# A hybrid two-layer decoder on one core: the order of transposes, products and low halves in the second layer's first norm

## Chip, cores and metric

One Trainium2 chip, one of its cores. The metric is the device time of one launch in microseconds (us), as the median of several runs. A second number appears beside it: the span of one profiled execution, from its first instruction to its last, which is a little shorter than that execution's own time.

## What is computed

512 tokens of width 1024 go through two layers, each a mixer and a mixture of experts, each with a norm ahead and a residual sum behind. The place of the change is the seam between the two layers:

```
h = rms_norm(x, norm_ffn_w[0])
x = x + hierarchical_moe(h, ...)      # each token: two experts, two weights
h = rms_norm(x, norm_mix_w[1])
mix = retention_mixer(h, ...)         # begins with h @ w_in, 1024 x 6144
```

All products are in float32 accuracy: each operand is split into a rounded high part and the low part that is left, and three matmuls (high by high, low by high, high by low) replace one.

## The kernel before

The kernel is written engine by engine, in one fixed order for each; engines meet only at semaphores. The tokens are 4 tiles of 128 (T = 0 to 3). Weights come as pieces: SyncE loads 512 KB, ScalarE makes the high half (L1006), GpSimd or VectorE the low half (L840, L1761).

**The seam, step by step.** Each token's two expert results lie in HBM, scattered there by GpSimd. ScalarE issues the loads of them, tile by tile (L1343 to L1346). For each tile these steps follow:

1. VectorE adds the two weighted results into the residual `x`: `combine`, two instructions (L1469). The second raises `moe_added0`.
2. TensorE waits for that, and transposes the tile: 8 transposes of 128x128 into two PSUM banks (L2144).
3. ScalarE writes the high half of the transposed tile, scaled with the norm's weights: 8 instructions of 128x128 (`transposed`, L1029). It also sums the squares of the tile's rows (`square`, L1020).
4. VectorE writes the low half: 8 instructions (`lo_tiles`, L1572). The first four can start once ScalarE's first four are done, since the two banks are handed over one by one.
5. TensorE multiplies the tile with the first weight block of the retention input (`rows(10, T)`): four pieces of 6 matmuls each, 24 in all (L673 to L675). It waits for the whole low half of the tile.

The norm's root isn't applied here; it is applied to the products later on, so the products don't wait for it. The roots are made while the products run: GpSimd turns each sum of squares into a root (L855, L856), ScalarE makes four diagonal matrices of them (`roots`, L1062), issues three small loads (L1370), prepares three weight pieces (L1006) and then evacuates the first block's products (L1242), followed by VectorE (L1820). The next block's first product waits for that.

**Orders around the change.** A tile's low half is L(T), its combines C(T), its transposes X(T), its products of pieces 0 to 2 P(T), of piece 3 Q(T). TensorE's order before is: 22 filler matmuls, X0, X1, 3 fillers, P0, X2, Q0, P1, X3, Q1, then P2 Q2 P3 Q3, roots. The fillers (`keep_busy`, L2111; each is two matmuls in the trace) compute nothing that is used. VectorE's order is C0 C1 L0 C2 L1 C3 L2 L3. ScalarE's is: high halves of 0, of 1, square 0, high halves of 2, square 1, high halves of 3, squares 2 and 3.

Each `hT` tile takes two of four PSUM banks in turn (`open_tile`), so a tile's transposes also wait until the low half of the tile two before it has been made.

Of the kernel before, what the change touches and what calls it, by code (L numbers as in the profile page):

```python
# [32 lines left out]
NT = SEQ // P  # L33
# [33 lines left out]
MOE_AT = (10, 26)  # L67
# [4 lines left out]
def first_piece(db):  # L72

    return 4 * db + (6 * NE if db >= MOE_AT[0] else 0)
# [248 lines left out]
def build(nc, a, out):  # L323
    ctx = ExitStack()
    with ctx:
# [3 lines left out]
        def sem(name):  # L329
            return ctx.enter_context(nc.semaphore(name))  # L330
# [39 lines left out]
        def v3(ap, k):  # L370
            return ap.rearrange("p (k n) -> p k n", k=k)
# [119 lines left out]
        def fin(T):  # L491
            return reg(DM * T, DM)
# [19 lines left out]
        def s_(name):  # L512
            if name not in SEM:
                SEM[name] = sem(name)
            return SEM[name]
# [90 lines left out]
        def tile(name):  # L606
            return ps[:, 4 + SIDE_AT[name] % 4, :]

        def tile_is_ready(eng, name):
            eng.wait_ge(tile_ready, SIDE_AT[name] + 1)  # L610
# [57 lines left out]
        def cols(T, w=P):  # L668
            return slice(T * w, T * w + w)
# [327 lines left out]
        def _(act):  # L997
# [24 lines left out]
            def transposed(n, T):  # L1022
                for g in range(2):
                    name = ("hT", n, T, g)
                    tile_is_ready(act, name)
                    if n == 2:
                        for j in range(4):
                            k = 4 * g + j
                            A(act.activation(HTH[:, k, cols(T)], tile(name)[:, cols(j)], ACT.Copy, scale=nw1[:, k:k + 1]),  # L1029
                              s_("hT_hi_made") if j == 3 else None)  # L1030
                        continue
                    A(act.activation(HTH[:, 4 * g:4 * g + 4, cols(T)], v3(tile(name), 4), ACT.Copy), s_("hT_hi_made"))

            def norm(n):
                if n == 2:
                    act.wait_ge(s_("wb_loaded"), 32)
                    transposed(n, 0)
                    for T in range(NT):
                        if T + 1 < NT:
                            transposed(n, T + 1)  # L1040
                        square(n, T)
                    roots()
                    return
                if n == 4:
                    for T in range(NT):
                        square(n, T)
                    return
                for T in range(3):
                    square(n, T)
                transposed(n, 0)  # L1050
                hi(0)
                square(n, 3)
                transposed(n, 1)
                transposed(n, 2)
                hi(1)
                transposed(n, 3)
                hi(2)
# [383 lines left out]
        def _(dve):  # L1441
# [24 lines left out]
            def combine(l, T, j):  # L1466

                dve.wait_ge(s_("yp_second0" if T == 0 and j == 1 else f"yp_loaded{T}"), 16 * (l + 1))
                D(stt(X[:, T, :], YP[:, T, j, :], w12[:, 2 * T + j:2 * T + j + 1], X[:, T, :], ALU.mult, ALU.add),  # L1469
                  s_(f"moe_added{l}") if j == 1 else None)  # L1470

            def norm(n):
                if n == 2:
                    for i in range(4):
                        lo(first_piece(10) + i)
                    combine(0, 0, 0)
                    combine(0, 0, 1)
                    combine(0, 1, 0)
                    combine(0, 1, 1)
                    dve.wait_ge(s_("wb_loaded"), 32)  # L1480
                    for T in range(NT):
                        lo_tiles(("hT", n, T), T)
                        if T + 2 < NT:
                            combine(0, T + 2, 0)
                            combine(0, T + 2, 1)
                    return
                if n == 4:
                    def last(T):
                        dve.wait_ge(s_("norm_r"), 16 + T + 1)
                        D(stt(fin(T), X[:, T, :], rs[:, T:T + 1], wb(4), ALU.mult, ALU.mult), s_("fin_dve"))  # L1490

                    for T in range(NT):
                        for j in range(2):
                            combine(1, T, j)
                        if T == 2:
                            dve.wait_ge(s_("wb_loaded"), 64)
                            last(0)
                    last(1)
                    last(2)
                    dve.wait_ge(s_("norm_r"), 16 + 4)  # L1500
                    for hf in range(2):
                        c = slice(512 * hf, 512 * hf + 512)
                        D(stt(fin(3)[:, c], X[:, 3, c], rs[:, 3:4], wb(4)[:, c], ALU.mult, ALU.mult), s_("fin_dve"))
                    return
                def scale(T):
                    dve.wait_ge(s_("norm_r"), T + 1)
                    D(stt(htok(0)[:, T, :], X[:, T, :], rs[:, T:T + 1], wb(0), ALU.mult, ALU.mult), s_("h_ready"))

                dve.wait_ge(s_("wb0_loaded"), 16)
                scale(0)  # L1510
                scale(1)
                lo_tiles(("hT", n, 0), 0)
                scale(2)
                lo_tiles(("hT", n, 1), 1)
                scale(3)
                lo_tiles(("hT", n, 2), 2)
                lo_tiles(("hT", n, 3), 3)
# [45 lines left out]
            def lo_tiles(name, T):  # L1563

                for g in range(2):
                    nm = name + (g,)
                    dve.wait_ge(s_("hT_hi_made"), hT_hi_count(nm))
                    hi, lo = (x[:, 4 * g:4 * g + 4, cols(T)] for x in ((HTH2, HTL2) if name[0:3] == ("yT", 1, 0) else (HTH, HTL)))
                    if name[0:2] == ("hT", 2):
                        for j in range(4):  # L1570
                            k = 4 * g + j
                            ins = stt(lo[:, j, :], tile(nm)[:, cols(j)], nw1[:, k:k + 1], hi[:, j, :].bitcast(F32), ALU.mult, ALU.subtract)  # L1572
                            if j < 3:
                                D(ins)
                            else:
                                D.read(ins, nm)
                    elif name[0:2] == ("yT", 0):
                        D.read(stt(lo, v3(tile(nm), 4), head_w[:, g:g + 1], hi.bitcast(F32), ALU.mult, ALU.subtract), nm)
                    else:
                        D.read(tt(lo, v3(tile(nm), 4), hi.bitcast(F32), ALU.subtract), nm)  # L1580
# [506 lines left out]
        def _(pe):  # L2087
# [20 lines left out]
            def keep_busy(count):  # L2108

                for _ in range(count):  # L2110
                    mm(ps[:, 0, 0:5 * CH], ident[:, :], gm.rearrange("p m t -> p (m t)"), start=True, stop=True)  # L2111
# [18 lines left out]

            def norm(n):
                if n == 2:
                    keep_busy(22)
                for T in range(NT):
                    if n == 2:
                        pe.wait_ge(*x_ready(n, T))
                    else:
                        pe.wait_ge(s_("h_ready"), h_count(n, T))
                    row = X[:, T, :] if n == 2 else htok(n)[:, T, :]
                    for g in range(2):  # L2140
                        t = open_tile(("hT", n, T, g))
                        for j in range(4):
                            k = 4 * g + j
                            ins = tr(t[:, cols(j)], row[:, k:DM:KD], ident[:, :])  # L2144
                        done(ins)
                    if n == 0 and T < 2:
                        stay_warm((4, 6)[T])
                    if n == 0 and T == 2:
                        stay_warm(4)
                        piece0(0, (0, 1))  # L2150
                    if n == 2:
                        if T == 1:
                            keep_busy(3)
                        if T > 1:
                            rows(MOE_AT[0], T - 2, (3,))
                        if 0 < T < NT - 1:
                            rows(MOE_AT[0], T - 1, (0, 1, 2))
                if n == 0:
                    piece0(0, (2, 3))
                    piece0(1, (0, 1, 2, 3)).then_inc(piece_used, 1)  # L2160
                if n == 2:
                    rows(MOE_AT[0], 2)
                    rows(MOE_AT[0], 3)

            def roots():
                pe.wait_ge(s_("rs_diag"), NT)
# [648 lines left out]
```

## Time and profile before

| | |
|---|---|
| median of 3 runs | 1178.06 us (1177.57 to 1178.78) |
| the profiled execution's own time | 1180.1 us |
| its span | 1178.3 us |
| TensorE busy | 1111.0 us, 94% |
| mean granted TensorE clock | 0.974 of full |
| VectorE, ScalarE, GpSimd busy | 59%, 52%, 34% |

The rows below write an engine as PE (TensorE matmuls), PEld (its weight loads), DVE (VectorE), ACT (ScalarE), POOL (GpSimd), SP (SyncE). L2144 is line 2144 of the kernel. In a timeline, one row merges equal instructions that follow one another: start, duration of the whole row, engine, line, operation, output and inputs, count; in square brackets the idle time of the engine ahead of it and what ended that. Matmul ends are modelled, so a matmul's rate is read from the starts of two that follow each other.

### The profile page before, as it was taken

What the parts mean: (1) busy time and instruction counts of PE and PEld (TensorE: products, weight loads), DVE (VectorE), ACT (ScalarE), POOL (GpSimd) and SP (SyncE); (2) the same over time, 40 slices, a digit from 0 to 9 for tenths busy, and PEclk for the clock granted to TensorE, in tenths of its full rate; (3) what the DMA queues carried; (4) which work ended last, traced back from release to release, by engine and by line L of the source; (5) the groups of instructions that cost most, each with busy time, mean ns of one, the idle gap of its engine ahead of it and who ended that gap; (6) DMA issues with size and microseconds to landing.
All of it is one profiled execution on the core that took longest, in us unless ns stands there. A gap on an engine that the chain in (4) does not pass through costs nothing.

```text
span 1178.3 us, 19724 instructions
## 1 busy us (share of the span) xinstructions
PE 1111.0 (94%) x7062; PEld 912.4 (77%) x7063; DVE 699.3 (59%) x1016; ACT 608.7 (52%) x903; POOL 395.7 (34%) x344
## 2 busy tenths in 40 slices
PE   8999999999998899998999999999999997999990
PEld 5778887778787688886788888888888886788870
DVE  5435444368736999996646341543432138999975
ACT  5556234242434699995633342233342234899971
POOL 4343221110133244332155325442234442344332
PEclk8999999999999899999999999999999998999995
DMA  9333311112225699996443213331222364999945
GB/s 263 77 88 55 73 38 55 36 41 70 72 64 210 244 358 379 382 365 225 181 128 98 81 56 106 94 108 58 81 73 90 98 198 161 355 381 377 381 191 223
DMA packets 81668, 194.76 MB, mean 165 GB/s; under 512 B 20349, under 2 KB 21433, under 8 KB 80825
## 3 DMA queue, kind: packets, MB, share of 16 engines
q1 hardware_dynamic: 59368, 159.34, 40.2%
q10 hardware_dynamic: 12432, 17.60, 4.4%
q0 software_dynamic: 9792, 16.80, 3.8%
q8 instruction: 49, 0.80, 0.3%
q14 instruction: 27, 0.21, 0.1%
HBM read 189.50 MB, written 23.07 MB: 180 GB/s over the span
## 4 chain that ended last, share of the span: by engine, by line
PE 83%; DVE 7%; DMA 3%; ACT 3%; issue 1%; ACTq 1%; POOL 0%; POOLq 0%; DVEq 0%
PE ps L673 24%; PE ps L675 23%; PE ps L674 23%; PE ps L2572 2%; PE ps L2364 2%; DMA arena<-y 1%; DVE x L1469 1%; PE ps L2247 1%; ACTq L1423 1%; PE ps L2500 1%; DMA arena<-hs,slot_rows 1%; PE ps L2637 1%; PE ps L2201 1%; ACT wh L1006 1%; DMA y<-arena,cur_rows 1%
## 5 line engine op out<-in xcount | busy, mean ns | idle before, releaser
L840 POOL TENSOR_TENSOR wl<-raw,wh 128x1024 fp32r<-128x1024 f32 x94 | 228.6, 2440 | 380.4 <-ACT wh L1006 380.1
L673 PE MATMUL ps<-wh,hT_hi 128*128 128x512 f32 x864 | 347.3, 402 | 2.9 <-DVE hT_lo L1988 2.4
L675 PE MATMUL ps<-wh,hT_lo 128*128 128x512 f32 x864 | 338.4, 392 | 0.0
L674 PE MATMUL ps<-wl,hT_hi 128*128 128x512 f32 x864 | 337.9, 391 | 0.0
L1006 ACT ACTIVATE wh<-raw 128x1024 fp32r<-128x1024 f32 x116 | 122.4, 1068 | 213.0 <-PE ps L675 191.3
L673 PEld LDWEIGHTS ps<-wh,hT_hi 128*128 128x128 f32 x864 | 163.1, 189 | 38.1 <-DVE hT_lo L1988 2.9
L675 PEld LDWEIGHTS ps<-wh,hT_lo 128*128 128x128 f32 x864 | 162.6, 188 | 34.5
L674 PEld LDWEIGHTS ps<-wl,hT_hi 128*128 128x128 f32 x864 | 163.0, 189 | 30.7
L673 PE MATMUL ps<-hT_hi,wh 128*128 128x512 f32 (+1 forms) x296 | 117.0, 395 | 2.0 <-DVE arena_rounded L1820 1.0
L1963 DVE TENSOR_TENSOR wl<-arena,wh 128x1024 fp32r<-128x1024 f32 x96 | 113.6, 1222 | 5.6 <-ACT wh L1293 5.3
L674 PE MATMUL ps<-hT_lo,wh 128*128 128x512 f32 (+1 forms) x296 | 114.5, 387 | 0.0
L675 PE MATMUL ps<-hT_hi,wl 128*128 128x512 f32 (+1 forms) x296 | 114.4, 387 | 0.0
L1963 DVE TENSOR_TENSOR wl<-raw,wh 128x1024 fp32r<-128x1024 f32 x92 | 109.2, 1223 | 7.7 <-ACT wh L1293 6.2
L1293 ACT ACTIVATE wh<-arena 128x1024 fp32r<-128x1024 f32 x94 | 98.4, 1070 | 6.9 <-PE ps L675 5.8
L1293 ACT ACTIVATE wh<-raw 128x1024 fp32r<-128x1024 f32 x84 | 88.1, 1072 | 5.2 <-PE ps L675 4.1
L673 PEld LDWEIGHTS ps<-hT_hi,wh 128*128 128x128 f32 x296 | 56.0, 189 | 15.7 <-issue 2.0
L675 PEld LDWEIGHTS ps<-hT_hi,wl 128*128 128x128 f32 x296 | 56.1, 189 | 11.4
L674 PEld LDWEIGHTS ps<-hT_lo,wh 128*128 128x128 f32 x296 | 56.0, 189 | 10.3
L885 POOL COPY cur_rows<-slot_rows 128x1 uint32 (+1 forms) x32 | 6.6, 206 | 139.6 <-PE ps L2572 139.6
L851 POOL TENSOR_TENSOR small<-small 128x4 f32<-128x4 f32 (+1 forms) x10 | 14.5, 1448 | 98.4 <-DVE small L1699 98.4
L1955 DVE TENSOR_TENSOR hT_lo<-ps,hT_hi 128x512 fp32r<-128x512 f32 x64 | 41.1, 683 | 0.6 <-ACT hT_hi L1351 0.5
L1020 ACT ACTIVATE arena<-x 128x1024 f32<-128x1024 f32 x20 | 21.2, 1058 | 37.3 <-DVE x L1469 18.2
(331 smaller groups left out, 1581.1 us busy)
## 6 DMA issues: line engine op xcount, KB each, us to landing
raw<-in_moe_w_gate_up_dram SPq DMA_DIRECT2D x64, 512.0 KB, 9.7
arena<-in_moe_w_gate_up_dram SPq DMA_DIRECT2D x64, 512.0 KB, 9.6
raw<-in_odd_w_in_dram SPq DMA_DIRECT2D x48, 512.0 KB, 3.8
raw<-in_even_w_in_dram SPq DMA_DIRECT2D x32, 512.0 KB, 4.8
arena<-in_moe_w_down_dram SPq DMA_DIRECT2D x32, 512.0 KB, 10.1
raw<-in_moe_w_down_dram SPq DMA_DIRECT2D x32, 512.0 KB, 12.8
raw<-in_odd_w_out_dram SPq DMA_DIRECT2D x16, 512.0 KB, 3.5
arena<-y ACTq DMA_DIRECT2D x6, 1024.0 KB, 9.8
```

The costliest lines, as they stand in the source:

```text
L673: nc.tensor.matmul(dst, lh, rh, start=first, stop=False)
L674: nc.tensor.matmul(dst, lh, rl, start=False, stop=False)
L675: return nc.tensor.matmul(dst, ll, rh, start=False, stop=last)
L840: pool.tensor_tensor(columns_of(i, wl[:, i % NSPL, :, :]), raw_columns(i), columns_of(i, wh[:, i % NSPL, :, :]).bitcast(F32), ALU.subtract ...
L851: pool.tensor_tensor(dst, src, mhalf[:, 0:n], ALU.pow).then_inc(on, 1)
L1006: act.activation(columns_of(i, wh[:, i % NSPL, :, :]), raw_columns(i), ACT.Copy).then_inc(hi_done, 1)
L1020: A(act.activation(squares(n), X[:, T, :], ACT.Square, scale=DM ** -0.5, accum_out=ss[:, T:T + 1]), s_("norm_ss"))
L1293: act.activation(wh[:, n % NSPL, :, :], raw_at(in_turn(n, it)), ACT.Copy).then_inc(hi_done, 1)
L1955: tt(HTL[:, 2 * par + g, :], ps[:, 4 + g, :], HTH[:, 2 * par + g, :].bitcast(F32), ALU.subtract).then_inc(s_("xT_lo"), 1)
L1963: tt(wl[:, n % NSPL, :, :], raw_at(in_turn(n, it)), wh[:, n % NSPL, :, :].bitcast(F32), ALU.subtract).then_inc(lo_dve, 1)
L2364: blocks(name, lambda o, b, n: mm(o, of_block(lh, b, n), of_block(rh, b, n), start=True, stop=True))
L2572: ins = tr(ps[:, 4 + g, cols(j)], xg[:, par, 4 * g + j:DM:KD], ident[:, :])
```

## The change

VectorE makes the low half of tile 0 right after tile 0's combines, ahead of tile 1's. TensorE no longer transposes tile T+1 ahead of tile T's products: it runs pieces 0 to 2 of tile T-1, then tile T's transposes, then piece 3 of tile T-1. ScalarE takes the square of a tile right after that tile's high halves. The fillers become 20 and 5 in place of 22 and 3.

```diff
@@ ScalarE
                     act.wait_ge(s_("wb_loaded"), 32)
-                    transposed(n, 0)
                     for T in range(NT):
-                        if T + 1 < NT:
-                            transposed(n, T + 1)
+                        transposed(n, T)
                         square(n, T)
                     roots()
@@ VectorE
-                    combine(0, 0, 0)
-                    combine(0, 0, 1)
-                    combine(0, 1, 0)
-                    combine(0, 1, 1)
-                    dve.wait_ge(s_("wb_loaded"), 32)
                     for T in range(NT):
-                        lo_tiles(("hT", n, T), T)
-                        if T + 2 < NT:
-                            combine(0, T + 2, 0)
-                            combine(0, T + 2, 1)
+                        combine(0, T, 0)
+                        combine(0, T, 1)
+                        dve.wait_ge(s_("wb_loaded"), 32)
+                        if T > 1:
+                            lo_tiles(("hT", n, T - 1), T - 1)
+                        elif T == 0:
+                            lo_tiles(("hT", n, 0), 0)
+                    lo_tiles(("hT", n, NT - 1), NT - 1)
                     return
@@ TensorE
                 if n == 2:
-                    keep_busy(22)
+                    keep_busy(20)
                 for T in range(NT):
+                    if n == 2 and T > 0:
+                        rows(MOE_AT[0], T - 1, (0, 1, 2))
                     if n == 2:
                         pe.wait_ge(*x_ready(n, T))
@@
                     if n == 2:
-                        if T == 1:
-                            keep_busy(3)
-                        if T > 1:
-                            rows(MOE_AT[0], T - 2, (3,))
-                        if 0 < T < NT - 1:
-                            rows(MOE_AT[0], T - 1, (0, 1, 2))
+                        if T == 0:
+                            keep_busy(5)
+                        else:
+                            rows(MOE_AT[0], T - 1, (3,))
@@
                 if n == 2:
-                    rows(MOE_AT[0], 2)
-                    rows(MOE_AT[0], 3)
+                    rows(MOE_AT[0], NT - 1)
```

TensorE's order is now: 20 fillers, X0, 5 fillers, P0, X1, Q0, P1, X2, Q1, P2, X3, Q2, P3 Q3, roots. Its queue at the start of the seam, before (L2111 are the fillers, L2144 the transposes, L673 the first product of a tile):

```order
L2111 MATMUL ps<-half_masks,ident 128x320 x22
L2144 MATMUL ps<-ident,x 128x128 x16
L2111 MATMUL ps<-half_masks,ident 128x320 x3
L673 MATMUL ps<-wh,hT_hi 128x512
L674 MATMUL ps<-wl,hT_hi 128x512
L675 MATMUL ps<-wh,hT_lo 128x512
```

and with the change, where the fillers stand at L2108 and the transposes at L2143:

```order
L2108 MATMUL ps<-half_masks,ident 128x320 x20
L2143 MATMUL ps<-ident,x 128x128 x8
L2108 MATMUL ps<-half_masks,ident 128x320 x5
L673 MATMUL ps<-wh,hT_hi 128x512
L674 MATMUL ps<-wl,hT_hi 128x512
L675 MATMUL ps<-wh,hT_lo 128x512
```

Tile 1's 8 transposes have gone from ahead of the first product to behind the 18th; those of tiles 2 and 3 each moved behind 24 more products than before.

VectorE's queue in the seam, before (L1469 are the combines, L1572 the low halves, L1820 the next block's):

```order
L1469 SCALAR_TENSOR_TENSOR x<-arena,small,x 128x1024 x4
L1572 SCALAR_TENSOR_TENSOR hT_lo<-ps,vec,hT_hi 128x128 x8
L1469 SCALAR_TENSOR_TENSOR x<-arena,small,x 128x1024 x2
L1572 SCALAR_TENSOR_TENSOR hT_lo<-ps,vec,hT_hi 128x128 x8
L1820 SCALAR_TENSOR_TENSOR arena_rounded<-ps,small,arena_rounded 128x512 x4
```

and with the change (L1467 the combines, L1569 the low halves, L1817 the next block's):

```order
L1467 SCALAR_TENSOR_TENSOR x<-arena,small,x 128x1024 x2
L1569 SCALAR_TENSOR_TENSOR hT_lo<-ps,vec,hT_hi 128x128 x8
L1467 SCALAR_TENSOR_TENSOR x<-arena,small,x 128x1024 x4
L1569 SCALAR_TENSOR_TENSOR hT_lo<-ps,vec,hT_hi 128x128 x8
L1817 SCALAR_TENSOR_TENSOR arena_rounded<-ps,small,arena_rounded 128x512 x4
```

Only one group moved: the low half of tile 0 and the combines of tile 1 have changed places. From tile 1's low half on, the two queues are the same.

## Rows read from the trace of the kernel before

**Rows 1.** The page's chain that ended last, by engine.
```profile
PE 83%; DVE 7%; DMA 3%; ACT 3%; issue 1%; ACTq 1%; POOL 0%; POOLq 0%; DVEq 0%
```

**Rows 2.** Chain of waits through the seam's start: start, us, what.
```profile
551.89 8.31 DMA arena<-y
...
560.29 1.30 DVE x L1469
```

**Rows 3.** Timeline of the seam, PE, DVE and ACT.
```profile
548.11 12.11 PE L2111 MATMUL ps<-half_masks,ident 128*128 128x320 f32 x44 [1.83 <-issue]
...
556.54 2.60 DVE L1469 SCALAR_TENSOR_TENSOR x<-arena,small,x 128x1024 f32<-128x1024 f32 x2 [4.01 <-DMA arena<-y]
...
560.06 1.04 PE L2144 MATMUL ps<-ident,x 128*128 128x128 f32 x8
...
562.93 3.06 DVE L1572 SCALAR_TENSOR_TENSOR hT_lo<-ps,vec,hT_hi 128x128 fp32r<-128x128 f32 x8
...
562.95 1.16 PE L2144 MATMUL ps<-ident,x 128*128 128x128 f32 x8 [1.85 <-DVE x L1469]
...
566.04 0.50 PE L673 MATMUL ps<-wh,hT_hi 128*128 128x512 f32 x1 [0.32 <-DVE hT_lo L1572]
...
570.28 1.04 PE L2144 MATMUL ps<-ident,x 128*128 128x128 f32 x8
...
571.07 0.48 PE L673 MATMUL ps<-wh,hT_hi 128*128 128x512 f32 x1
...
576.64 1.04 PE L2144 MATMUL ps<-ident,x 128*128 128x128 f32 x8
577.34 3.17 ACT L1029 ACTIVATE hT_hi<-ps,vec 128x128 fp32r<-128x128 f32 x8 [2.01 <-PE ps L2144]
...
579.00 3.11 DVE L1572 SCALAR_TENSOR_TENSOR hT_lo<-ps,vec,hT_hi 128x128 fp32r<-128x128 f32 x8 [1.55 <-ACT hT_hi L1029]
```

**Rows 4.** Timeline behind the last tile's high halves, up to the next block's first product.
```profile
581.71 1.06 ACT L1020 ACTIVATE arena<-x 128x1024 f32<-128x1024 f32 x1
...
583.90 1.71 ACT L1062 ACTIVATE arena<-ident,small 128x128 f32<-128x128 f32 x4 [1.03 <-POOL small L856]
...
587.05 3.17 ACT L1006 ACTIVATE wh<-raw 128x1024 fp32r<-128x1024 f32 x3 [1.44 <-issue]
...
589.79 1.05 PE L2169 MATMUL ps<-arena,small 128*128 128x128 f32 x8
590.12 2.84 ACT L1242 ACTIVATE arena_rounded<-ps,small 128x512 fp32r<-128x512 f32 x4
...
591.80 0.47 PE L673 MATMUL ps<-hT_hi,wh 128*128 128x512 f32 x1 [0.95 <-DVE arena_rounded L1820]
```

**Rows 5.** Timeline of PE at two idle stretches elsewhere.
```profile
314.48 0.66 PE L2527 MATMUL ps<-arena 64*64 64x128 f32 x8 [1.76 <-DVE state L1755]
...
991.40 1.68 PE L2572 MATMUL ps<-ident,arena 128*128 128x128 f32 x8 [2.02 <-DMA arena<-hs,slot_rows]
```

**Rows 6.** Windows of 1 us: PE busy, its instructions, granted clock, DMA share, GB/s.
```profile
316.00:317.00 1.00, 0.81 (x8) 0.51 0.05 20
992.00:993.00 1.00, 1.00 (x7) 0.50 0.14 57
562.00:563.00 1.00, 0.05 (x1) 1.00 0.84 352
```

**Rows 7.** Timeline of PE at half clock: first two products, and the first one behind.
```profile
80.72 0.63 PE L674 MATMUL ps<-hT_lo,wh 128*128 128x512 f32 x1
81.14 0.63 PE L675 MATMUL ps<-hT_hi,wl 128*128 128x512 f32 x1
...
84.03 0.39 PE L673 MATMUL ps<-hT_hi,wh 128*128 128x512 f32 x1
```

**Rows 8.** Window of 100 us behind the seam, PE, columns as in rows 6.
```profile
592.00:692.00 100.00, 100.00 (x456) 1.00 0.33 100
```

**Rows 9.** Waits of PE from 592 to 1150, the largest: us, times, longest.
```profile
PE ps L2227 <- DVE arena L1868: 3.0, 2, 2.6
```

## The prediction

> **What bounds the kernel now.** I read the page's chain first: TensorE holds 83% of it [rows 1], so outside the seam the kernel goes at TensorE's pace. Then the chain through the seam, where it leaves TensorE. It runs through the loads of the expert results, whose last link before the norm ends at 560.2, when tile 1's results are there [rows 2]; then through tile 1's combines (560.29 to 562.90), tile 0's low half (562.93 to 565.99) and on to the first product at 566.04 [rows 3]. So the first product waits for VectorE, which does tile 1's combines ahead of tile 0's low half. The change takes that away. From 566.04 TensorE never stops until 589.79, when it reaches the roots' matmuls [rows 3, 4].
>
> The reader should see two more things. **First, what hides a tile's latency.** From the start of a tile's transposes to its finished low half three engines work in turn. For the last tile, where nothing else is in the way: transposes at 576.64, ScalarE from 577.34 to 580.51, VectorE from 579.00 to 582.11 [rows 3]. That is 5.47 us, and with the 0.06 us from a low half's end to the product that waits for it 5.53 us. TensorE doesn't feel it now, because between tile T's transposes and its products stand 24 products of the two tiles before it. **Second, a second chain.** After the last transposes ScalarE has the high halves, two squares (the last starts at 581.71), the roots (583.90), three loads to issue, three weight pieces (587.05) and only then the first evacuation at 590.12, with the next block's first product at 591.80 [rows 4]. The pieces run back to back (3.17 us for three), so at the end of the seam it is ScalarE that is late, by the 0.95 us that TensorE waits there.
>
> **The terms.** A tile's first 18 products after a wait take 570.28 - 566.04 = 4.24 us [rows 3]. Behind transposes the first product starts 571.07 - 570.28 = 0.79 us after their start. From tile 3's transposes to the roots' matmuls stand 6 + 24 + 24 = 54 products, so one takes (589.79 - 576.64 - 0.79) / 54 = 0.229 us [rows 3, 4].
>
> *The start, a gain.* Tile 0's combines end at 559.14 [rows 3]. Before, its transposes came only at 560.06, held up by the 22 fillers (44 matmuls from 548.11, 0.27 us each). With 20 the fillers end at about 559.0, and the transposes start at 559.19 (the 0.05 us is what tile 1's show: combines end 562.90, transposes 562.95). Tile 0's low half is next in VectorE's queue, so the first product comes at 559.19 + 5.53 = 564.72. Gain so far: 566.04 - 564.72 = 1.32 us. The 5 new fillers take 10 x 0.27 = 2.7 us of this wait and leave some 1.8 us idle, as before (1.85 ahead of 562.95).
>
> *The low half and the combines, change places.* Combines of tile 1: about 564.7 to 567.3, of tile 2 to 569.9, of tile 3 behind tile 1's low half. Each tile is summed before its transposes' turn comes, as below. That the later low halves still stand behind a combine costs nothing: tile 1's can't start before 571.3, and VectorE is free at 569.9.
>
> *The transposes behind the products, the large term.* Tile T's transposes now start 4.24 us after tile T-1's first product. Between them and tile T's first product only 6 products stand. Transposes and these take 0.79 + 6 x 0.229 = 2.2 us, but the low half needs 5.53 us. TensorE idles 5.53 - 2.2 = 3.3 us, three times. A tile's period is 4.24 + 5.53 = 9.77 us, against 6.36 us before (576.64 - 570.28).
>
> | | transposes | first product |
> |---|---|---|
> | tile 0 | 559.19 | 564.72 |
> | tile 1 | 568.96 | 574.49 |
> | tile 2 | 578.73 | 584.26 |
> | tile 3 | 588.50 (before 576.64) | 594.03 |
>
> Tile 3's 24 products end at 594.03 + 0.11 + 24 x 0.229 = 599.6, where 589.79 was (0.11: what a first product after a wait takes longer).
>
> *The end of the seam.* ScalarE's chain hangs on tile 3's transposes, 11.86 us later. It gets one square back: tile 2's now stands ahead of tile 3's high halves, so the last square comes right behind them, 0.70 + 3.17 + 0.02 = 3.89 us after the start of the transposes, at 592.39: 10.68 us after its 581.71. Roots, loads and pieces follow as before, since none of the three pieces waits for TensorE longer: the last needs tile 3's piece 2 done at about 598.4, and ScalarE comes to it at 599.8. The next block's first product is at 591.80 + 10.68 = 602.48. TensorE's own path (599.6, then 1.05 us of roots' matmuls) is 1.8 us shorter, so ScalarE's decides. **Shift: +10.7 us**, at a full clock.
>
> *The clock.* Rows show the granted clock falling to half of full (1.2 in place of 2.4 GHz) around idle stretches of 1.76 and 2.02 us [rows 5, 6], and not around the 1.85 us ahead of 562.95 [rows 3, 6]. At half clock a product takes 81.14 - 80.72 = 0.42 us in place of 0.23; that stretch ended by 84.03, after (84.03 - 80.72) / 0.42 = some eight products [rows 7], and so cost 8 x 0.2 = 1.6 us. Each of the new stalls is longer than every one of these, so the clock will likely fall. Bounds: nothing, and 1.6 us for each fall. I take 1.2 us, nearer the upper end, since a fall that begins within the idle time has less work left to slow. Two of the three count (ahead of tile 1's and tile 2's products): the third delays tile 3's products alone, where TensorE has 1.8 us to spare. **+2.4 us.**
>
> The Trainium skill, page "TensorE: Matmul & The Clock Gate", section "Why this matters for your kernels", speaks against this change: it tells to leave no long idle gap between bursts of matmuls, because the array then goes back to half rate. By that rule both stalls on the path would be paid in full, 3.2 us in place of my 2.4, as in the second rival below. The trace agrees in part: of the three idle stretches named, two brought the clock down.
>
> *Behind the seam nothing gives it back.* TensorE is busy for 100.00 us of the next 100 [rows 8], and its waits up to the last experts are short and for VectorE, which moves along [rows 9]. The transfers of the expert results were issued before the seam and hang on nothing that moved; the weight loads wait for buffers that TensorE and GpSimd free, and so move with the rest.
>
> **Sum.** 10.7 + 2.4 = 13.1 us. The profiled execution took 1180.1 us and would take 1193.2; it lies 2.0 us above the median, so against the median: 1178.06 + 13.1 = **1191.2 us**.
>
> **Rivals.**
> - *Full clock.* The stalls come, the clock stays. For it: 1.85 us of idle time did nothing, with transposes on both sides. Against: 3.3 us is longer than all of those. 1178.06 + 10.7 = 1188.7.
> - *Both falls at full price.* Each fall begins only when the products run again, and slows some eight of them: 2 x 1.6 = 3.2 us, 1178.06 + 10.7 + 3.2 = 1192.0. For it: at 316 and 992 the clock was at half while TensorE was busy again [rows 6]. Against: the idle stretches here are longer, so more of the half clock may fall into them. (This is the time that the skill's rule gives.)
> - *Half clock throughout.* Once down, the clock doesn't recover within a tile. The 18 products ahead of the transposes of tiles 2 and 3 would take 18 x 0.2 = 3.6 us more each, the transposes a little too: 10.7 + 8 = 18.7, 1196.8. Against: a stretch at half clock ended after some eight products while TensorE stayed busy [rows 7], and a tile has 24.
> - *Not slower: the delay is taken up behind the seam.* If weights or buffers, not TensorE, set the pace of the retention blocks, work ahead would gather during the stalls, and TensorE would catch up. It decides where TensorE waits for at least 10.7 us, from 592 on, on something that doesn't move with it; then 1178.1, or 1176.7 with the early start. The rows have it at 0 in the next 100 us, and at 3.0 us for the largest of its later waits.
> - *The change doesn't reach what it says.* VectorE's queue changes in one place only, as its rows show. If that were all that counts, TensorE's earlier start would be the whole effect: -1.3 us, 1176.7. It would need a latency behind a tile's transposes below 2.2 us, where the rows have 5.53.
>
> **How the numbers follow.** Stalls with falls of the clock that are paid in part: 0.46, my forecast. Both at full price: 0.30. Full clock: 0.16. Half clock throughout: 0.03. Not slower, by either way: 0.04. The last 0.01 is for a large miss upwards. The range takes in full clock, less 1.2 us for my sum being made of single rows (1187.5), and reaches up to three falls on the path at full price (10.7 + 4.8 = 15.5) with 0.6 for the sum: 1194.2. Some 2 us, 0.2%, is about what a measurement of this kernel can tell from no change. Slower by more 0.96, within it 0.03, faster by more 0.01.
>
> **What the profile would show.** Right: first product at 564.7; three idle stretches of 3.3 us ended by the low half, so some 10 us of waits of TensorE's first product for it, where 0.3 stood; tile 3's transposes at 588.5 or up to 3 us later; the next block's first product at 602.5 to 605.5; windows at half clock between 570 and 600. Wrong: if TensorE's stalls are well below 3 us each, the latency of a tile isn't what I read; if the shift at the next block's first product is some 12 us but the time grows by less, something behind the seam had slack.

## The result, and the profile after

| | before | after |
|---|---|---|
| median | 1178.42 us (1177.57 to 1187.04, 4 runs) | 1195.15 us (1192.99 to 1197.99, 4 runs) |
| ratio after to before | | 1.0131, 95% interval 1.0105 to 1.0157 |
| span of the profiled execution | 1178.3 us | 1191.3 us |
| mean granted clock | 0.974 | 0.972 |

The change makes the kernel slower by 1.3%: 15.4 us by the ratio (12.4 to 18.5 by its interval), 16.7 us by the difference of the two medians. I forecast 13.1 us. On the 1178.06 us that I forecast from, the ratio gives 1193.5 us, inside my range; the plain median of the four runs lies 1.0 us above its upper end (1194.2). The four times stand in two pairs, 1193.0 and 1193.1 against 1197.2 and 1198.0; their mean clocks are 0.973 and 0.972 against 0.965 and 0.965. That is a first sign that the clock has a larger part in the time than my sum gave it.

The profiled execution took 1193.1 us, where I had put 1193.2. That is luck: its seam lost more than my sum said, and the rest of this execution took less, as the traces show next.

The timeline of the seam after the change, all engines (columns as in rows 3 and 4; the whole trace stands 2.8 us earlier here, see below):

```profile
553.75 2.61 DVE L1467 SCALAR_TENSOR_TENSOR x<-arena,small,x 128x1024 f32<-128x1024 f32 x2 [4.23 <-DMA arena<-y]
...
556.42 1.16 PE L2143 MATMUL ps<-ident,x 128*128 128x128 f32 x8 [0.29 <-DVE x L1467]
...
562.06 0.50 PE L673 MATMUL ps<-wh,hT_hi 128*128 128x512 f32 x1 [1.79 <-DVE hT_lo L1569]
...
566.30 1.04 PE L2143 MATMUL ps<-ident,x 128*128 128x128 f32 x8
...
571.84 0.80 PE L673 MATMUL ps<-wh,hT_hi 128*128 128x512 f32 x1 [3.10 <-DVE hT_lo L1569]
...
578.82 1.05 PE L2143 MATMUL ps<-ident,x 128*128 128x128 f32 x8
...
584.36 0.61 PE L673 MATMUL ps<-wh,hT_hi 128*128 128x512 f32 x1 [3.10 <-DVE hT_lo L1569]
...
590.20 1.05 PE L2143 MATMUL ps<-ident,x 128*128 128x128 f32 x8
590.90 3.17 ACT L1029 ACTIVATE hT_hi<-ps,vec 128x128 fp32r<-128x128 f32 x8 [7.03 <-PE ps L2143]
...
595.74 0.80 PE L673 MATMUL ps<-wh,hT_hi 128*128 128x512 f32 x1 [3.10 <-DVE hT_lo L1569]
...
605.68 0.47 PE L673 MATMUL ps<-hT_hi,wh 128*128 128x512 f32 x1 [0.56 <-DVE arena_rounded L1817]
```

The reader should see three first products, each with 3.10 us of idle time ahead of it that a low half ends. In [rows 3, 4] TensorE ran from 566.04 to the roots without a stop. TensorE's waits in the seam say the same in one row (us in total, times, longest), where [rows 3] had 0.32 us:

```profile
PE ps L673 <- DVE hT_lo L1569: 11.1, 4, 3.1
```

To compare traces that begin the seam at different times I measure from the start of tile 0's transposes to the next block's first product, **the stretch** from here on: 591.80 - 560.06 = 31.74 us before, 605.68 - 556.42 = 49.26 us after. My table had 602.48 - 559.19 = 43.3 us for it at full clock. What lies between 43.3 and 49.3 is the clock, as experiments 2 and 3 show. Windows of 1 us of TensorE after the change (length, busy time and instructions, granted clock, DMA share, GB/s), at the first and at the second of the three stalls:

```profile
570.00:571.00 1.00, 0.00 (x0) 0.97 1.05 385
571.00:572.00 1.00, 0.16 (x1) 0.50 0.99 365
...
576.00:577.00 1.00, 1.00 (x4) 0.50 0.00 0
577.00:578.00 1.00, 1.00 (x4) 0.62 0.00 0
...
584.00:585.00 1.00, 0.64 (x2) 0.80 0.02 8
585.00:586.00 1.00, 1.00 (x3) 0.50 0.00 0
...
587.00:588.00 1.00, 1.00 (x4) 0.50 0.00 0
588.00:589.00 1.00, 1.00 (x5) 1.00 0.00 0
```

The clock falls at 570.9, while TensorE is idle, and comes back at 577.8: 6.8 us. At the second stall it falls at 584.6, just after the products have started, and comes back at 588.0: 3.4 us.

**The rest of the trace.** The seam's first row stands at 553.75 in place of 556.54. The first layer lost less here: the two stretches that the clock spent at half there before, one from 80.7 to 84.0 [rows 7] and one at 316 [rows 6], aren't in this trace, though nothing was changed there. Behind the seam, from the next block's first product to the second layer's router (the matmul at L2227 before, L2223 after, that follows a wait of 0.46 us), it takes 976.52 - 591.80 = 384.72 us before and 990.40 - 605.68 = 384.72 us after. Nothing of the delay is given back up to there. The row before:

```profile
976.52 0.19 PE L2227 MATMUL ps<-arena 128*128 128x32 bf16 x1 [0.46 <-DVE arena L1868]
```

and after:

```profile
990.40 0.19 PE L2223 MATMUL ps<-arena 128*128 128x32 bf16 x1 [0.46 <-DVE arena L1865]
```

From there to the end it takes 201.8 us before and 200.9 us after. So the 13.0 us between the two spans are 2.8 us less ahead of tile 0's combines, 51.93 - 35.26 = 16.7 us more from these to the next block's first product, and 0.9 us less at the end.

### The profile page after: what moved, and what is told of

It reads as the page before. It is cut to its first block, busy times and chain, and to the rows that moved or that the text cites. A ratio compares the mean times of both kernels' runs of the same rounds, so it can differ in the third digit from the quotient of the medians.

```text
span 1191.3 us, 19726 instructions
## 1 busy us (share of the span) xinstructions
PE 1114.0 (94%) x7063; PEld 913.1 (77%) x7063; DVE 699.2 (59%) x1016; ACT 609.0 (51%) x903; POOL 397.5 (33%) x344
## 4 chain that ended last, share of the span: by engine, by line
PE 84%; DVE 7%; DMA 3%; ACT 2%; issue 2%; ACTq 1%; POOLq 0%; POOL 0%; DVEq 0%; SPq 0%
PE ps L673 24%; PE ps L675 23%; PE ps L674 23%; PE ps L2568 2%; PE ps L2360 2%; PE ps L2197 1%; DMA arena<-y 1%; DVE hT_lo L1569 1%; DVE x L1467 1%; PE ps L2243 1%; ACTq L1421 1%; DMA arena<-hs,slot_rows 1%; PE ps L2496 1%; DMA x<-in_x_dram 1%; PE ps L2633 1%
## 5 line engine op out<-in xcount | busy, mean ns | idle before, releaser
L673 PE MATMUL ps<-wh,hT_hi 128*128 128x512 f32 x864 | 349.8, 405 | 13.8 <-DVE hT_lo L1569 11.1
L673 PEld LDWEIGHTS ps<-wh,hT_hi 128*128 128x128 f32 x864 | 164.3, 190 | 51.0 <-DVE hT_lo L1569 12.9
L673 PE MATMUL ps<-hT_hi,wh 128*128 128x512 f32 (+1 forms) x296 | 116.3, 393 | 2.2 <-issue 0.9
L673 PEld LDWEIGHTS ps<-hT_hi,wh 128*128 128x128 f32 x296 | 55.6, 188 | 15.9 <-issue 2.2
```

The source lines that it names most:

```text
L673: nc.tensor.matmul(dst, lh, rh, start=first, stop=False)
```

## Experiments

Theory A, from the prediction: three stalls of some 3 us and the second chain, on ScalarE, cost 10.7 us, and the rest of the loss is TensorE's clock, which the stalls bring down. Each experiment's times are compared with runs of the kernel before that were taken together with them.

**1. The changed kernel again.** No edit.

> The changed kernel once more, for a second trace of the same program. Theory A (stalls of 3.1 us, three of them, and a clock that falls in each): the seam, from tile 0's combines to the next block's first product, takes 51.9 us as in the first trace if the clock falls at the same points, and down to 46.0 us (35.3 + 10.7) where it doesn't; run times come in groups some 3 to 5 us apart, with the mean clock lower in the longer ones. Rival B (the order alone costs all of it, whatever the clock): the seam is 51.9 us again within 0.3, and the groups come from elsewhere in the kernel.

1193.39 us (1192.43 to 1198.09, 4 runs), ratio 1.0118 (1.0079 to 1.0157). The stretch takes 604.05 - 557.74 = 46.31 us, 3 us less than in the first trace of the same program, with stalls of 3.09 us each. (From tile 0's combines, as I put it in advance, it is 50.4 us; there the second load of tile 0 came 1.5 us late, which is why I measure from the transposes.) What differs is the clock: two low stretches of 3.4 us, and none at the third stall. Rival B falls. An idle stretch of 3.09 us can leave the clock alone, as this trace shows at tile 3:

```profile
595.62 0.50 PE L673 MATMUL ps<-wh,hT_hi 128*128 128x512 f32 x1 [3.09 <-DVE hT_lo L1569]
```

```profile
593.00:594.00 1.00, 0.00 (x0) 1.00 0.00 0
594.00:595.00 1.00, 0.00 (x0) 1.00 0.00 0
596.00:597.00 1.00, 1.00 (x6) 1.00 0.00 0
```

**2. Fillers in the stalls.** The changed kernel, with 5 fillers into a PSUM bank that is free there, behind each tile's piece 3:

```diff
-            def keep_busy(count):
+            def keep_busy(count, bank=0):
...
-                    mm(ps[:, 0, 0:5 * CH], ident[:, :], ...)
+                    mm(ps[:, bank, 0:5 * CH], ident[:, :], ...)
...
                         else:
                             rows(MOE_AT[0], T - 1, (3,))
+                            keep_busy(5, 3)
```

> Fillers in the three stalls keep TensorE busy for 2.7 of 3.1 us, in the same order of the products; nothing else changes. Theory A: full clock from 560 to 606, tile 1's first product 9.8 us after tile 0's, the seam at 46.0 us, the kernel 10.7 to 11 us above before (1189.0 against 1178.2), and runs closer together. Rival B: the fillers change nothing, since the stalls are the waits for the low halves: the seam stays near 51.9 us and the kernel at 1193 to 1198.

1190.12 us (1187.79 to 1192.43, 6 runs), ratio 1.0078 (1.0053 to 1.0102): 9.2 us slower than before, with 6 to 12 in the interval. The stretch takes 603.29 - 559.92 = 43.37 us, with no window below full clock in it. So the loss at full clock is 43.4 - 31.7 = 11.6 us in this stretch, of which the earlier transposes of tile 0 (0.9 us) are taken off again: 10.7. That part of the sum stands to a tenth in the trace, and the runs' 9.2 us allow it. From tile 0's combines it is 603.29 - 554.37 = 48.9 us and not 46.0, since in this trace the 20 fillers began at half clock (from 547.5 to 551) and held tile 0's transposes back by 2.9 us. Rival B falls: the stretch is 3 to 6 us shorter than without fillers. The run times did not draw closer, which I had expected: they spread over 4.6 us here, and the kernel before over 7.8 us on this chip (1177.16 to 1184.99).

**3. Fewer fillers.** 3 in place of 5 in each stall, `keep_busy(3, 3)`.

> 3 fillers (1.6 us) in place of 5 in each of the three stalls, so that about 1.5 us of each stays idle, less than every idle stretch that has brought the clock down so far. Theory A: the clock stays full through the seam or falls once at most, and from tile 0's transposes to the next block's first product it takes 43.3 us as with 5 fillers (49.3 and 46.3 in the two traces without any). Rival D (any idle stretch ahead of products can bring the clock down, whatever its length): falls behind two or three of the stalls again, 45 to 49 us.

1189.84 us (1188.93 to 1190.67, 4 runs), ratio 1.0077 (1.0052 to 1.0102). Timeline and windows of TensorE in this kernel, at tile 1 and behind the last stall:

```profile
574.11 0.50 PE L673 MATMUL ps<-wh,hT_hi 128*128 128x512 f32 x1 [1.48 <-DVE hT_lo L1569]
...
602.06 0.47 PE L673 MATMUL ps<-hT_hi,wh 128*128 128x512 f32 x1 [1.84 <-DVE arena_rounded L1817]
```

```profile
574.11:578.33 4.22, 4.22 (x19) 1.00 0.05 17
593.60:602.06 8.46, 6.62 (x32) 1.00 0.31 95
```

The stretch takes 602.06 - 558.72 = 43.34 us at full clock throughout, and from tile 0's combines 602.06 - 556.05 = 46.01 us, where 35.3 + 10.7 = 46.0 had been put down. Idle stretches of 1.48 us, three in a row, left the clock alone. Rival D isn't borne out; experiment 7 gives three more such stretches.

**4. TensorE's order undone.** The changed kernel with the old `norm` on TensorE (22 fillers, X0, X1, 3 fillers, P0, X2, Q0, ...); VectorE and ScalarE as changed.

> TensorE's order as before (22 fillers, both transposes, 3 fillers, products), with the new orders of VectorE and ScalarE. Theory A: the loss is TensorE's order; here tile 1's transposes wait for tile 1's combines, now behind tile 0's low half, to about 567.4 on the clock of the first trace, and the first product comes near 569.9 against 566.04; no stalls behind it; the seam takes 38.2 us, 2.9 more than before, of 1181 us in all. Rival C (VectorE's new order is what costs, by holding back tiles 1 to 3): the seam stays above 45 us.

1186.37 us (1182.64 to 1188.29, 10 runs), ratio 1.0050 (1.0034 to 1.0067): 5.9 us slower than before, twice what I had expected. From tile 0's combines to the next block's first product it takes 596.47 - 555.52 = 40.95 us, where 38.2 was put down. TensorE's timeline and two of its windows in this kernel:

```profile
567.26 1.97 PE L2141 MATMUL ps<-ident,x 128*128 128x128 f32 x8 [7.13 <-DVE x L1467]
569.03 2.38 PE L2108 MATMUL ps<-half_masks,ident 128*128 128x320 f32 x6
571.00 0.64 PE L673 MATMUL ps<-wh,hT_hi 128*128 128x512 f32 x1
```

```profile
563.00:564.00 1.00, 0.00 (x0) 0.70 0.04 16
569.00:570.00 1.00, 1.00 (x4) 0.50 1.04 401
```

Tile 1's transposes come 8.17 us after tile 0's (8.16 by the sum), so what I had read of VectorE's order is right. The missing 2.75 us have three parts. TensorE is idle for 7.13 us ahead of them, the clock falls at 563.4 and is back at 570.2, and transposes and fillers take 3.74 us where my sum had 2.5: 1.2 us. I had worked that idle stretch out and not asked what it does to the clock. The 22 fillers hold tile 0's transposes to 3.57 us after its combines, as in the kernel before, where I had taken the 2.65 of 20 fillers: 0.9 us. And ScalarE's weight pieces wait for TensorE behind the last products, as in experiment 11: 0.6 us. No stalls follow, so rival C falls; yet it has a point: VectorE's new order fits only with TensorE's new one. With TensorE's old order, and ScalarE's new one, which alone shows in no run time (experiment 11), it costs 5.9 us.

**5. Transposes behind 6 products.** A tile's transposes stand behind piece 0 of the tile before, with pieces 1 to 3 behind them:

```diff
                     if n == 2 and T > 0:
-                        rows(MOE_AT[0], T - 1, (0, 1, 2))
+                        rows(MOE_AT[0], T - 1, (0,))
...
                         else:
-                            rows(MOE_AT[0], T - 1, (3,))
+                            rows(MOE_AT[0], T - 1, (1, 2, 3))
```

> A tile's transposes stand behind 6 of the products of the tile before it, in place of 18; 18 products follow them, in place of 6. Theory A: the stall shrinks from 3.1 us by 12 x 0.229 = 2.75 us to some 0.4 us for tiles 2 and 3 (tile 1's transposes also wait about 1.1 us for its combines), the clock stays full, tile 3's transposes come some 4.8 us later than before and the seam takes 35.3 + 3.6 = 38.9 us; kernel near 1182. Rival B' (it is enough that products stand ahead of transposes at all): the stalls stay near 3 us and the seam above 45 us.

1182.82 us (1179.51 to 1184.81, 10 runs), ratio 1.0015 (0.9999 to 1.0032). Timeline of TensorE in this kernel:

```profile
567.82 1.16 PE L2143 MATMUL ps<-ident,x 128*128 128x128 f32 x8 [0.99 <-DVE x L1467]
...
573.56 0.50 PE L673 MATMUL ps<-wh,hT_hi 128*128 128x512 f32 x1 [0.47 <-DVE hT_lo L1569]
...
580.62 0.50 PE L673 MATMUL ps<-wh,hT_hi 128*128 128x512 f32 x1 [0.39 <-DVE hT_lo L1569]
...
587.69 0.50 PE L673 MATMUL ps<-wh,hT_hi 128*128 128x512 f32 x1 [0.38 <-DVE hT_lo L1569]
```

The stalls are 0.47, 0.39 and 0.38 us where 0.4 was forecast, and tile 1's transposes wait 0.99 us for their combines where 1.1 was. The stretch takes 596.14 - 559.64 = 36.50 us (38.9 less the 2.65 us up to the transposes: 36.2 expected). From the combines it is 42.1 us, since the 20 fillers began at half clock in this trace and held tile 0's transposes back. So it is the number of products behind a tile's transposes that decides: 12 more of them take 2.7 us off each stall, and 10 us off the kernel, the clock's part with it. The stretch is still 36.50 - 31.74 = 4.8 us longer than before, 3.9 with tile 0's earlier transposes taken off; the runs show 1.8 us, with 0.1 faster to 3.8 slower in the interval. Why it is at the upper end of that stays open.

**6. VectorE's order undone, 5 fillers in each stall.** The `norm` of VectorE as before, the rest as in 2.

> As with 5 fillers in each stall, but VectorE's order as before: tile 1's combines ahead of tile 0's low half. Theory A: this order is worth the early start alone; from the start of tile 0's combines to tile 0's first product 9.5 us as in the kernel before (8.3 in the changed one), and three periods of 9.8 us behind it as with the new order. Rival C (VectorE's order has a part in the stalls): the periods come out shorter than 9.8 us.

One run, 1189.93 us. The periods between first products are 9.81, 9.79 and 9.80 us. The first term doesn't come out of this trace: the fillers began at half clock here too, held tile 0's transposes to 559.12, and the first product came 11.1 us after the combines, as in 2. Inconclusive for the early start, so I repeated it with 3 fillers.

**7. The same with 3 fillers in each stall.**

> 3 fillers in each stall, and VectorE's order as before the change (tile 1's combines ahead of tile 0's low half). Theory A: if the 20 fillers at the start run at full clock, tile 0's first product comes 9.5 us after its combines begin, as in the kernel before, where the new order had 8.3 us; three periods of 9.8 us behind it, and 44.6 us from tile 0's transposes to the next block's first product, 1.3 more than with the new order. Rival C (VectorE's order has a part in the stalls): periods below 9.8 us.

One run, 1191.38 us, at full clock through the seam. First product 564.26 - 554.78 = 9.48 us after the start of the combines; with the new order it was 562.06 - 553.75 = 8.31. The stretch takes 602.10 - 557.44 = 44.66 us, 1.3 more than in 3. Both as put down: the new place of tile 0's low half is worth 1.2 to 1.3 us, and no more. Rival C falls. The three stalls with fillers keep 1.49 us of idle time each, and the clock stays full again.

**8. to 10. Three more traces of the changed kernel**, for a rule on the clock that the first two traces suggested.

> The changed kernel, one more look at its three stalls. From two traces: a stall of 3.1 us brings the clock down five times in six; where it falls within 0.5 us of the first product or behind it, the low stretch lasts 3.2 to 3.5 us and the 18 products take 5.6 to 5.8 us in place of 4.2; where it falls 0.8 us or more ahead of the first product, the low stretch lasts 6.6 us and they take 7.0 us. Theory F: the same rule holds in this trace, for each stall. Rival G: the long stretches come without regard to where the clock fell.

> As the look before, the same two theories: 5.6 to 5.8 us for 18 products behind a late fall, 7.0 us behind an early one, 4.2 us without one (F), or no such order (G).

> As the two looks before, the same two theories (F and G), with the same numbers.

1197.69, 1192.22 and 1197.43 us. All fifteen stalls of the five traces of this program, with the time at which the clock fell, against the first product behind the stall (read from windows of 0.2 us), and how long it stayed at half:

| trace | tile 1 | tile 2 | tile 3 | the stretch |
|---|---|---|---|---|
| first | 0.90 ahead, 6.8 us | 0.24 behind, 3.4 us | 0.90 ahead, 6.8 us | 49.26 us |
| again | 0.66 behind, 3.4 us | 0.45 ahead, 3.4 us | no fall | 46.31 us |
| again2 | 1.05 ahead, 6.8 us | 0.15 behind, 3.4 us | 0.97 ahead, 6.8 us | 49.14 us |
| again3 | 0.39 ahead, 3.4 us | no fall | 0.85 ahead, 6.8 us | 46.34 us |
| again4 | 0.03 ahead, 3.4 us | 1.13 ahead, 6.8 us | 0.11 behind, 3.4 us | 47.92 us |

Thirteen falls in fifteen stalls. Every fall that came 0.85 us or more ahead of the first product lasted 6.8 us, every other one 3.4. Theory F holds in all, G falls. What a fall costs shows between a first product and the next transposes, which is 4.22 to 4.27 us without one: 5.60 to 5.84 us behind a short fall, 6.87 to 6.98 behind a long one. So 1.4 to 1.6 us, or 2.6 to 2.8. Behind the last stall, windows over the stretch to the next block's first product, in the first trace:

```profile
595.74:605.68 9.94, 9.38 (x32) 0.70 0.38 117
```

Against the 8.46 us of kernel 3 a long fall there costs 1.5 us; a short one cost 0.3 (608.04 - 599.27 = 8.77 in the last trace). How it gets through, in ScalarE's timeline of the first trace:

```profile
599.43 1.13 ACT L1006 ACTIVATE wh<-raw 128x1024 fp32r<-128x1024 f32 x1 [1.44 <-PE ps L675]
601.32 1.14 ACT L1006 ACTIVATE wh<-raw 128x1024 fp32r<-128x1024 f32 x1 [0.76 <-PE ps L675]
602.97 1.14 ACT L1006 ACTIVATE wh<-raw 128x1024 fp32r<-128x1024 f32 x1 [0.51 <-PE ps L675]
```

The three weight pieces no longer run back to back as in [rows 4]; the second and the third wait 0.76 and 0.51 us for TensorE's products of tile 3 that free their buffers, and the evacuation is queued behind them.

**11. One part of the change put into the kernel before.** ScalarE alone: tile 2's square ahead of tile 3's high halves.

```diff
-                    transposed(n, 0)
-                    for T in range(NT):
-                        if T + 1 < NT:
-                            transposed(n, T + 1)
-                        square(n, T)
+                    transposed(n, 0)
+                    transposed(n, 1)
+                    for T in range(NT):
+                        if T == 3:
+                            transposed(n, T)
+                        square(n, T)
+                        if T == 0:
+                            transposed(n, 2)
```

> The kernel before, with one thing of the change: ScalarE takes the square of tile 2 ahead of tile 3's high halves instead of behind them. Theory A: ScalarE's chain at the end of the seam gets 1.2 us shorter, TensorE's becomes the longer one, and the next block's first product comes 0.9 us earlier (30.8 us after tile 0's transposes in place of 31.7); the kernel 0.9 us faster, less than the runs can tell. Rival E (ScalarE's chain isn't what the next block waits for): nothing moves, 31.7 us.

1178.84 us (12 runs), ratio 0.9990 (0.9974 to 1.0006). The stretch takes 591.43 - 560.09 = 31.34 us, 0.4 us less than before; I had put down 0.9. ScalarE in this kernel:

```profile
585.99 1.12 ACT L1006 ACTIVATE wh<-raw 128x1024 fp32r<-128x1024 f32 x1 [1.54 <-PE ps L675]
587.35 1.14 ACT L1006 ACTIVATE wh<-raw 128x1024 fp32r<-128x1024 f32 x1 [0.24 <-PE ps L675]
588.71 1.14 ACT L1006 ACTIVATE wh<-raw 128x1024 fp32r<-128x1024 f32 x1 [0.22 <-PE ps L675]
```

The pieces wait for TensorE again, and the evacuation behind them gains only part of the 1.2 us. The chain is the one I named, so rival E falls, but the time is no different from before by what the runs can tell. No version here beats the kernel before clearly.

## Why the prediction was right, and where it was too small

The mechanism was right: three stalls for the low half, ScalarE's chain at the end, and a clock that falls. One term of the sum was too small, the clock's.

- **The early start.** Forecast 1.32 us, measured 9.50 - 8.31 = 1.19. Right. The missing 0.1 us: ScalarE's first high half starts 557.23 - 556.42 = 0.81 us after transposes that follow idle time, not 0.70 as after the others.
- **The stalls.** Forecast three of 3.3 us, measured three of 3.10. From a tile's transposes to its first product 5.53 us forecast, 5.54 measured (571.84 - 566.30); the period 9.77 us forecast, 9.75 at full clock (574.11 - 564.36 in kernel 3). Right.
- **ScalarE's chain as the one that ends last.** Forecast 43.3 us for the stretch at full clock, measured 43.34 and 43.37. Right, and with the early start taken off, 10.7 us. (Between a tile's transposes and its products stood 24 products before the change only for tile 1; for tiles 2 and 3 it was 30. The prediction's 24 enters no sum.)
- **Nothing is given back behind.** 384.72 us before and after, and 384.7 to 384.8 in every other trace. The rival on the other side falls.
- **The clock.** Here my sum failed. The step was "I take 1.2 us, nearer the upper end, since a fall that begins within the idle time has less work left to slow". The five traces show the reverse: a fall well ahead of the products is the dear one, since the clock then stays low for 6.8 us, and it costs 2.7 us, more than the 1.6 that I had as the upper bound. A short fall costs 1.5. The bound came from one low stretch of 3.3 us [rows 7], and in the 3 us ahead of it TensorE had no idle time, but ran 64 matmuls of one column each. The second step, "the third delays tile 3's products alone, where TensorE has 1.8 us to spare", held for a short fall (0.3 us) but not for a long one (1.5 us), because ScalarE's weight pieces wait for these same products. The prediction says that these pieces don't wait for TensorE, which by its own numbers holds only up to some 1.4 us of delay (599.8 against 598.4). In place of 2.4 us the clock took 5.9, 3.0, 5.8, 3.0 and 4.6 us in the five traces (the stretch less 43.3), 4.5 on the mean.
- **The size.** 10.7 + 4.5 = 15.2 us, against the 15.4 that the ratio of the first runs gives and 13.9 by the second (experiment 1).
- **The two groups of times** are these falls only in small part. The two long traces (1197.4 and 1197.7 us) have spans 5.0 us above the three short ones (1192.2 to 1193.1) on the mean: 3.1 us of it lie ahead of tile 0's transposes, 1.2 in the stretch and 0.7 behind. Between 20 and 360 us, in code that the change doesn't touch, the clock falls twice in each of the long ones, once in two of the short ones and never in the third.
- **The rule of the Trainium skill**, to leave no long idle gap between bursts of matmuls ("TensorE: Matmul & The Clock Gate", section "Why this matters for your kernels"), stood beside the rival of 1192.0 us, nearer than my own 1191.2. The traces agree with the rule in thirteen of fifteen stalls of 3.1 us; six shorter ones of 1.48 and 1.49 us left the clock alone. The rival's price of 1.6 us a fall fits the short falls (1.4 to 1.6); no rival had the long ones.

## What to carry to other kernels

When work is moved behind other work on the busiest engine, add up the whole latency of what follows it on the other engines (here 5.53 us over three engines), and count what is left to cover it; starting one tile 1.2 us sooner isn't worth uncovering that latency three times. The order before had at least 24 products between a later tile's transposes and its own products, and by my estimate needed no more than some 21 of them ((5.53 - 0.79) / 0.229).

Price an idle stretch on TensorE twice: for itself, and for the clock. Here the second was 4.5 us on top of the 10.7 of the first, and a few fillers in the stall, which compute nothing, took it away: in four traces with fillers the clock fell in none of twelve stalls.

## What I had not expected of the hardware

- The clock stays at half for 3.4 us or for 6.8 us, never between, in the thirteen falls; it was 6.8 us whenever TensorE stayed idle for another 0.85 us or more after the fall, and 3.4 us where that was 0.45 us or less. The one fall in experiment 4, 3.9 us ahead of the next matmul, lasted 6.8 us too.
- The same idle stretch of 3.1 us, fifteen times, left the clock alone twice. So two executions of one program differ by up to 3 us in this seam alone, and two traces have to be compared over a stretch that no such fall touches, or with the falls counted, all along the kernel.
- The clock also falls where nothing was changed, and not in every trace: twice in the first layer between 20 and 360 us in the trace before, not there in the first one after, and two to none in the five traces of the changed kernel. The seam began 2.8 us earlier in that first trace for a reason that has nothing to do with the change. What decides it isn't shown.
